# Memory queries by 512-column matmuls, their two halves joined by ScalarE and VectorE

## What is computed

```
def memory_cross_attention(h, mem_n, w_q, w_kv, w_o):      # h = rms_norm(x, norm_mem_q[l])
    q = (h @ w_q).reshape(b, s, MEM_HEADS, MEM_HEAD_DIM)   # 256 x 4 x 128
    kv = (mem_n @ w_kv).reshape(b, m, 2, MEM_HEADS, MEM_HEAD_DIM)
    k, v = kv[:, :, 0], kv[:, :, 1]
    sc = jnp.einsum('bqhd,bmhd->bhqm', q, k) * (MEM_HEAD_DIM ** -0.5)
    p = jax.nn.softmax(sc, axis=-1)
    o = jnp.einsum('bhqm,bmhd->bqhd', p, v).reshape(b, s, MEM_WIDTH)
    return o @ w_o
```

## Time and profile before

| | us |
|---|---|
| median of 3 runs | 1898.95 |
| lowest, highest | 1898.93, 1899.52 |
| the profiled execution | 1898.83 |
| its span in the trace | 1897.0 |

### The profile page before, as it was taken

How to read it: one execution, slowest core, us unless ns; L and a number is a source line. 1 busy time by engine, 2 the same in 40 slices (tenths; PEclk the granted TensorE clock), 3 DMA queues, 4 the chain that set the end, 5 groups by cost and what they waited for, 6 DMA issues and landing times.

```text
span 1897.0 us, 29616 instructions
## 1 busy us (share of the span) xinstructions
PE 1888.6 (100%) x11184; PEld 1631.7 (86%) x11184; DVE 1459.0 (77%) x2602; ACT 1174.0 (62%) x2167; POOL 394.0 (21%) x448
## 2 busy tenths in 40 slices
PE   9999999999999999999999999999999999999999
PEld 8889988887898888888988788888888897878887
DVE  7877996687799769866787978756885687897874
ACT  6767775567678656545667565545554666756552
POOL 2210211011011005411022214402440112123430
PEclk9999999999999999999999999999999999999999
DMA  9344566543455656555542355555555544345563
GB/s 368 123 134 143 198 204 223 166 155 122 134 190 193 206 172 204 190 193 182 177 162 94 119 189 189 191 192 184 190 191 193 182 155 151 104 144 181 189 194 127
DMA packets 91117, 331.96 MB, mean 175 GB/s; under 512 B 10080, under 2 KB 10592, under 8 KB 90592
## 3 DMA queue, kind: packets, MB, share of 16 engines
q1 hardware_dynamic: 90976, 330.08, 52.8%
HBM read 328.99 MB, written 1.05 MB: 174 GB/s over the span
## 4 chain that ended last, share of the span: by engine, by line
PE 91%; DVE 4%; ACT 3%; DMA 1%; issue 1%; SPq 0%; ACTq 0%; DVEq 0%
PE PS L83 88%; PE PS L86 3%; DVE TMP L108 1%; DVE WL L98 1%; ACT WH L92 1%; ACT TMP L95 1%; DVE SM L114 1%; DMA RAW<-wts 1%; DMA TMP<-xt 0%; ACT TMP L92 0%; ACT M L92 0%; DVE SM L108 0%; DVE SM L98 0%; DVE TMP L98 0%; DVE M L108 0%
## 5 line engine op out<-in xcount | busy, mean ns | idle before, releaser
L98 DVE TENSOR_TENSOR WL<-RAW,WH 128x1024 fp32r<-128x1024 f32 (+1 forms) x610 | 760.5, 1253 | 283.1 <-ACT WH L92 279.7
L92 ACT ACTIVATE WH<-RAW 128x1024 fp32r<-128x1024 f32 (+1 forms) x610 | 640.3, 1053 | 316.0 <-PE PS L83 310.6
L83 PE MATMUL PS<-HX,WH 128*128 128x512 f32 (+1 forms) x1920 | 523.4, 344 | 0.4
L83 PE MATMUL PS<-WH,GX 128*128 128x512 f32 (+1 forms) x1636 | 523.6, 391 | 0.0
L83 PE MATMUL PS<-HX,WL 128*128 128x256 f32 x1488 | 413.9, 281 | 0.0
L83 PE MATMUL PS<-GX,WH 128*128 128x256 f32 (+1 forms) x1776 | 409.5, 330 | 0.4
L83 PEld LDWEIGHTS PS<-HX,WH 128*128 128x128 f32 x1920 | 331.0, 189 | 46.6 <-DVE TMP L108 1.1
L83 PEld LDWEIGHTS PS<-WH,GX 128*128 128x128 f32 x1636 | 306.2, 188 | 63.0 <-issue 2.4
L83 PEld LDWEIGHTS PS<-GX,WH 128*128 128x128 f32 x1776 | 298.0, 190 | 30.5 <-DVE TMP L108 1.1
L83 PE MATMUL PS<-WL,GX 128*128 128x512 f32 (+1 forms) x818 | 317.0, 387 | 0.0
L98 POOL TENSOR_TENSOR TMP<-TMP,RB 128x256 f32<-128x256 f32 x176 | 204.9, 1169 | 474.8 <-DVE TMP L98 235.3
(11 more groups left out here) (146 smaller groups left out, 1701.2 us busy)
## 6 DMA issues: line engine op xcount, KB each, us to landing
RAW<-wts SPq DMA_DIRECT2D x607, 512.0 KB, 4.3
M<-bias SPq DMA_DIRECT2D x4, 512.0 KB, 12.1
M<-bias SPq DMA_DIRECT2D x1, 2048.0 KB, 10.2
X<-x SPq DMA_DIRECT2D x2, 512.0 KB, 10.7
M<-mem SPq DMA_DIRECT2D x1, 1024.0 KB, 12.8
M<-memt SPq DMA_DIRECT2D x1, 1024.0 KB, 11.8
CST<-cst SPq DMA_DIRECT2D x1, 794.0 KB, 12.2
out<-X SPq DMA_DIRECT2D x3, 256.0 KB, 4.5
```

Of the source, the lines that this page charges most:

```text
L83: return Issued(self.eng and self.eng.matmul(o, l, r, start=first, stop=last, skip_group_check=share))
L92: return Issued(self.eng.activation(o, i, f, scale=scale))
L98: return Issued(self.eng and self.eng.tensor_tensor(o, a, b, op))
```

## The change

The query tiles are made by `fm_four_halves` instead of `fm_four`: 32 steps of one 512-column and one 256-column matmul. ScalarE copies the second half of each tile's bank into MQ (`aout`), and VectorE adds the first half to it (`joined`); the scores wait for `joined`. `fm_four_halves` itself now takes the bank of a tile at the tile's first step instead of all four at the start, and for "mq" it puts the transposes before tile 3, as before; elsewhere before tile 2, also as before. For "mq" `turn_x` may now use all eight banks.

```diff
@@ mem_heads
-                               q_by=(aout, ("mq", L, h)), k_by=(aout, ("mk", L, h)), v_by=("mv", L),
+                               q_by=(joined, ("mq", L, h)), k_by=(aout, ("mk", L, h)), v_by=("mv", L),
@@ pe_program, fm_four_halves
-                ps = [take(k, WHOLE + STB) for k in keys]
+                ps = []
                 HALF[keys[0], 0] = at[0] // 8
                 for part in range(2):
                     for n in range(4):
-                        if part == 0 and n == 2:
+                        if part == 0:
+                            ps.append(take(keys[n], WHOLE + STB))
+                        if part == 0 and n == (3 if st[0] == "mq" else 2):
                             turn_x(st, 1, by, WHOLE + STB)
@@ pe_program, block1
-                fm_four([("mq", L, m) for m in range(4)], mq, ("mq", L), lambda c, t: (xnew, (("wo2", L), c, t)),
-                        WHOLE + STB)
+                fm_four_halves([("mq", L, m) for m in range(4)], mq, halves_of(side), ("mq", L),
+                               lambda c, t: (xnew, (("wo2", L), c, t)))
@@ act_program, block1
                 for m in range(4):
-                    out(MQ[:, m, :], ("mq", L, m))
+                    key = ("mq", L, m)
+                    highs(key)
+                    e.wait_ge(tile, key)
+                    e.act(ACT.Copy, MQ[:, m, :], bank(key)[:, S:2 * S]).then_inc(aout, key)
@@ dve_program, block1
                 norm(("mq", L))
                 for m in range(4):
-                    lows(("mq", L, m))
+                    key = ("mq", L, m)
+                    lows(key)
+                    e.wait_ge(aout, key)
+                    e.tt(MQ[:, m, :], MQ[:, m, :], bank(key)[:, 0:S], ALU.add).then_inc(joined, key)
```

## The result

The changed kernel takes 1901.78 us (median of 22 runs, 1901.5 to 1902.57), the kernel before in the same session 1899.22 (1898.8 to 1899.79): a ratio of 1.0014, 95% interval 1.0008 to 1.0020. That is 2.56 us more, where the forecast was 1.92 more. The profiled execution took 1902.14 us, with a span of 1900.2.

What follows compares the result with a forecast made beforehand. TensorE, busy 1888.6 of 1897.0 us, was taken as the bound. 1898.83 + 2 x 0.96 = 1900.75, with 0.12 for the median 1900.87; prediction 1900.8, own range 1900.2 to 1901.4 (80%), 8 in 10 of everything 1899.8 to 1902.0.

Steps and rivals of the forecast that it cites:

- Part 1: Query stage on TensorE: one matmul and weight load fewer a step, reaching the scores 0.37 us earlier in each layer.
- the rule that was weighed there: Skill page's fixed cost of about 2.5 ns a matmul: the query stage only 0.08 us shorter; trace preferred.
- Part 2: ScalarE's query tile copies: four 128x256 tiles as before, nothing added, tile 1 done at 131.92.
- Part 3: Scores wait for VectorE's second addition behind two pieces of lows: stop of 1.27 us, 0.96 us lost a layer.
- the wake: Time from the end of VectorE's addition to TensorE's start on the scores, taken as 0.05 us.
- Part 4: After the scores start: VectorE about 0.2 us late at the maxima, swallowed by ScalarE's 1.92 us idle; cost nothing.
- Part 5: Banks taken one by one, transposes getting other banks: cost nothing, bounded by 0.1 us in total.
- The wait is not seen: Rival at the scores: no stop, the matmuls' gain stays, 1898.1 us; chance 6%.
- The lateness runs on: Rival: VectorE's lateness at the softmax reaches TensorE, 0.2 to 0.6 us a layer, 1901.2 to 1902.0; chance 8%.
- The clock falls: Rival: TensorE leaves the scores' stop at half pace, losing 3.2 us a layer, 1907.2; chance 4%.
- The halves bring nothing in this stage: Rival: query steps stay at 0.36 us, each layer loses 0.11 more, 1901.0; counted with the forecast, no own chance.

Runs made afterwards that it cites:

- e4: Changed kernel without VectorE's additions, the scores waiting for ScalarE's copies and one product missing from the queries: 1898.74 us, ratio 0.9998.
- e1: Changed kernel with tiles 0 and 1 added right behind norm, ahead of all pieces of lows, tiles 2 and 3 behind the third piece: 1900.22 us.
- e2: Changed kernel with tiles 0 and 1 added right behind norm, then two pieces, tiles 2 and 3, and the third piece behind the maxima: 1899.12 us.
- e5: Kernel before with the bank change alone, banks taken one by one and transposes from all eight: 1899.15 us, ratio 1.0001.
- e3: Changed kernel with all four additions behind all three pieces of lows: 1906.02 us, ratio 1.0037.
- e6: e2 with four memsets of one spare column each at VectorE's start, and tile SS widened for them: 1898.59 us, ratio 0.9998.
- e8: Changed kernel with additions in the order tile 1, 2, 0 ahead of the third piece and tile 3 behind it: 1902.39 us, ratio 1.0019.
- e9: Changed kernel with additions in the order tile 1, 2, 3, 0, all ahead of the third piece, which follows the maxima: 1903.11 us, ratio 1.0021.

## Why the prediction was right, and where it was off

- **Part 1, the matmuls.** The direction was right, the size a little too large: 0.32 us a layer (e4) instead of 0.37. As forecast, none of it reaches the end while VectorE is late. On the rule that was weighed there, 0.08 us a stage, the trace decides: 0.32. The transposes came 0.10 us earlier, where 0.11 was forecast.
- **Part 2.** ScalarE's copies were never what anyone waited for.
- **Part 3, the term that decides.** Less the 0.69 of the head, each time can be set against its forecast: lows at 132.04 (forecast 132.04), first addition 134.31 (134.32), second one ends at 135.06 (135.07), scores 135.21 (135.12). The chain on VectorE was right to 0.01 us. The mis-sized term is the wake: from the addition's end to TensorE's start it took 0.15 us in both layers, 0.05 in the row that I had taken it from the earlier trace rows. Coming out of the stop cost 0.08 and not 0.06. Together 0.21 us for both layers: 2.13 instead of 1.92. These are the terms of the sum that were mis-sized.
- **Part 4, the cover.** The result was right, since the maxima started 1.64 us behind the scores, only 0.08 more than before, and ScalarE's idle time at the memory values was 1.90 us after 1.92. But the reason was too generous: that idle time lies behind the second scores. With the maxima 1.33 us late, TensorE was 0.60 us late at them in e1, so the cover is about 0.7 us (an estimate); at 0.1 us (e2) there was no stop.
- **Part 5, the banks.** Nothing, shown by e5.
- **What the sum lacked.** 0.29 us at 508, from the eight additional instructions on VectorE, whoever waits for them. And the head: ahead of the first changed instruction the nine profiled kernels with 64 matmuls fewer are 0.05 to 0.76 us later than the trace of before (0.69, 0.19, 0.05, 0.34, 0.52, 0.76, 0.31, 0.29, 0.47; mean 0.40), the four of the old form -0.07 to 0.06. The steps arise at about 22 and 32 us, where TensorE waits for the weights' low pieces. Nothing in the instruction lists differs there, and one execution each is little; whether this belongs to the form is open. The medians don't ask for it in this pair: the difference of 2.56 less the 2.48 behind the head leaves 0.08 for the head and all else. Worked out in the same way, the other kernels with 64 matmuls fewer leave -0.04 to 0.52 and those of the old form -0.18 to 0.68.
- **How the sum closes.** The forecast of the median, 1900.87, lay 0.91 us too low. The base accounts for 0.27: it was 1898.95 from three runs, where the session of the comparison gave 1899.22. The mis-sized terms of part 3 are 0.21, the step at 508 is 0.29, small steps are 0.06, and 0.08 is left. The measured time lies above the range of 1900.2 to 1901.4 that the forecast had of its own. It lies within 1899.8 to 1902.0 because that range had room for lateness that runs on, which did not happen. That the total was met there is luck in part; the mechanism and its 2 us were not.
- **The rivals.** "The wait is not seen": refuted by the two stops. "The lateness runs on": its time, 1901.2 to 1902.0, was met, but not its mechanism; between the stop and 508 the shift does not grow. "The clock falls": not at 1.15 us; e3 shows the mechanism, behind a stop of 2.28 us and not behind one of 2.21, and 1.66 us as its price for one layer, half of the 3.2 that I had put on it. "The halves bring nothing in this stage": refuted by the 0.32 us a layer of e4.

The edit could have gained 0.64 us at most. It gave up this and 2.13 more, since the additions were put behind two pieces that nobody waits for at that time. With them moved ahead (e2, e6) it can't be told from the kernel before.

## What to carry to other kernels

Where a change gives the last step of a tile from an idle engine to a busy one, read what stands ahead of the new step in that engine's list: here 2.28 us of uncritical work stood ahead of two additions that take 0.75 us together, and the time at which they end followed from these two rows to 0.01 us. Put the step that others wait for first, and then look at the next thing the engine feeds, since the delay moves there (e1). When a kernel has its bottleneck engine busy for 99%, an instruction more on another engine can show up at a far place; so test a suspect step by adding harmless instructions at the start.

## What the runs showed of the hardware

- VectorE had gaps of 0.40 us (0.04 is usual between such updates) at two places of its instruction stream, records 191 and 831. With eight memsets in idle time, one came up at the update of X ahead of 508; with four, the same gap went. It cost TensorE 0.29 us there, and nothing at the other place.
- The granted clock held at 1.00 behind stops of 1.15, 1.31, 1.39, 1.65, 1.74 and 2.21 us, and fell to 0.50 behind one of 2.28 us, for three scores matmuls and five of 512 columns, which cost 1.66 us.
- A stop of TensorE of 1.15 us costs 0.08 us more on the way out: its first eight matmuls of 256 columns are shown with 1.97 us where it was 1.89. A stop of 0.42 us (e1) costs the same 0.08.
- From VectorE's addition to TensorE's start it took 0.15 us in the changed kernel and in e3, three times what it took behind the multiply-add of the earlier trace rows; in e8 and e9, with three and four additions ahead, it was 0.05 to 0.06, and the way out cost 0.11 instead of 0.08. Why it differs was not tried.
